# Value product of split probabilities in two passes instead of three, GpSimd's low parts spread, fillers of one attention regrouped

## What is computed

```python
def fox_branch(qb, kb, vb, log_f):
    ...
        logits = jnp.einsum('bqhd,bshd->bhqs', q_blk, kb).astype(jnp.float32) * scale
        logits = logits + jnp.transpose(cq_blk, (0, 2, 1))[..., None] - c_k[:, :, None, :]
        logits = jnp.where(causal[None, None], logits, NEG)
        probs = jax.nn.softmax(logits, axis=-1).astype(vb.dtype)
        return jnp.einsum('bhqs,bshd->bqhd', probs, vb)

def first_block(...):
    ...
    y_a = (att_a * jax.nn.silu(gate_a)) @ w_branch_a[i]
    y_b = (att_b * jax.nn.silu(gate_b)) @ w_branch_b[i]
    m_a, m_b = jnp.split(jax.nn.sigmoid(h @ w_merge[i]), 2, axis=-1)
    out = (m_a * y_a + m_b * y_b) @ w_out[i]
    x = x + rmsnorm(out, g_post[i])
    ...

def second_block(...):
    ...
    o_a = swa_sink_attention(qa, ka, va, swa_sinks[l])
    o_b = mla_attention(q_nope, q_rope, k_nope, k_rope, vb)
    y = jax.nn.sigmoid(g_a) * (o_a @ w_o_swa[l]) + jax.nn.sigmoid(g_b) * (o_b @ w_o_mla[l])
    x = x + y @ w_out[l]
    h = rmsnorm_2(x, ffn_norm_g[l])
    x = x + (jax.nn.silu(h @ w_gate[l]) * (h @ w_up[l])) @ w_down[l]
```

## Time and profile before

| | us |
|---|---|
| median of 3 runs | 1270.14 (1269.06 to 1270.3) |
| the profiled execution | 1270.64 |
| its span | 1268.8 |
| PE busy | 1223.2 (96%) |
| PE weight loads (beside PE) | 1020.5 (80%) |
| DVE busy | 618.7 (49%) |
| ACT busy | 539.7 (43%) |
| POOL busy | 532.7 (42%) |

### The profile page before, as it was taken

The page is one execution under the profiler, slowest core; times in us unless marked ns, Lnnn a source line. Parts: engine busy times, 40 slices in busy tenths (PEclk is TensorE's granted clock), DMA queues, the critical chain, the costliest instruction groups (busy, mean ns, idle before and its releaser), DMA issues.

```text
span 1268.8 us, 15954 instructions
## 1 busy us (share of the span) xinstructions
PE 1223.2 (96%) x6002; PEld 1020.5 (80%) x6002; DVE 618.7 (49%) x1455; ACT 539.7 (43%) x970; POOL 532.7 (42%) x284
## 2 busy tenths in 40 slices
PE   9989899999999989699899999999999999999997
PEld 8868688888888878499789777888788888888886
DVE  5499565673628264874863575582422222130003
ACT  6443473466523354445673466533332222222112
POOL 1436554435443433234353475334344443434441
PEclk9999999999999999799999999999999999999999
DMA  8303661302322423133112300423323233322221
GB/s 263 100 1 117 172 177 67 99 2 67 116 100 67 166 99 100 33 136 118 34 38 67 100 13 22 166 100 100 100 67 102 98 100 100 100 100 97 88 98 67
DMA packets 71115, 119.20 MB, mean 94 GB/s; under 512 B 5624, under 2 KB 33144, under 8 KB 70656
## 3 DMA queue, kind: packets, MB, share of 16 engines
q1 hardware_dynamic: 71040, 118.19, 28.5%
HBM read 107.67 MB, written 4.21 MB: 88 GB/s over the span
## 4 chain that ended last, share of the span: by engine, by line
PE 84%; DVE 7%; POOL 3%; issue 2%; ACT 1%; SPq 1%; DMA 0%; DVEq 0%; ACTq 0%; POOLq 0%
PE bank L1583 63%; PE bank L1865 9%; PE bank L1664 4%; PE bank L1632 2%; PE bank L1646 2%; PE bank L1708 2%; DVE sc L1313 1%; POOL w_lo L665 1%; DVE m L1309 1%; PE bank L1608 1%; DVE tmp L1373 1%; POOL sc L679 1%; ACT w_hi L765 0%; PE bank L1602 0%; SPq L581 0%
## 5 line engine op out<-in xcount | busy, mean ns | idle before, releaser
L648 POOL TENSOR_TENSOR w_lo<-w_raw,w_hi 128x2048 fp32r<-128x2048 f32 (+4 forms) x87 | 383.9, 4412 | 606.7 <-ACT w_hi L732 564.8
L1583 PE MATMUL bank<-aH,w_hi 128*128 128x512 f32 x800 | 318.3, 398 | 9.5 <-DVE aL L1385 3.9
L1583 PE MATMUL bank<-aH,w_lo 128*128 128x512 f32 x800 | 312.9, 391 | 0.0
L1583 PE MATMUL bank<-aL,w_hi 128*128 128x512 f32 x800 | 312.6, 391 | 0.0
L732 ACT ACTIVATE w_hi<-w_raw 128x2048 fp32r<-128x2048 f32 (+4 forms) x83 | 151.8, 1829 | 278.6 <-PE bank L1583 180.7
L1583 PEld LDWEIGHTS bank<-aH,w_hi 128*128 128x128 f32 x800 | 151.1, 189 | 40.1 <-issue 10.9
L1583 PEld LDWEIGHTS bank<-aH,w_lo 128*128 128x128 f32 x800 | 150.5, 188 | 32.4
L1583 PEld LDWEIGHTS bank<-aL,w_hi 128*128 128x128 f32 x800 | 150.9, 189 | 26.5
L1583 PE MATMUL bank<-w_hi,aH 128*128 128x512 f32 (+4 forms) x224 | 78.2, 349 | 7.1 <-ACT aH L961 6.6
L1071 DVE TENSOR_TENSOR fg<-bank,rB 128x512 f32<-128x512 f32 x22 | 15.1, 691 | 127.3 <-PE bank L1583 127.2
L1583 PE MATMUL bank<-w_lo,aH 128*128 128x512 f32 (+4 forms) x224 | 76.6, 342 | 0.0
(11 more groups left out here) (308 smaller groups left out, 2144.7 us busy)
## 6 DMA issues: line engine op xcount, KB each, us to landing
w_raw<-in_w_in SPq DMA_DIRECT2D x23, 1024.0 KB, 5.0
w_raw<-in_w_gate SPq DMA_DIRECT2D x22, 512.0 KB, 3.9
w_raw<-in_w_up SPq DMA_DIRECT2D x22, 512.0 KB, 4.8
w_raw<-in_w_down SPq DMA_DIRECT2D x11, 1024.0 KB, 4.8
w_raw<-in_w_merge SPq DMA_DIRECT2D x8, 1024.0 KB, 4.9
w_raw<-in_w_out SPq DMA_DIRECT2D x8, 1024.0 KB, 5.0
w_raw<-in_w_ple_gate SPq DMA_DIRECT2D x4, 1024.0 KB, 4.8
fK<-kbT SPq DMA_DIRECT2D x24, 128.0 KB, 2.6
```

The costliest lines, as they stand in the source:

```text
L648: pool.tensor_tensor(out=w_lo[:, c % 2, 0:n], in0=w_raw[:, c % 2, 0:n], in1=w_hi[:, c % 2, 0:n].bitcast(F32), op=ALU.subtract).then_inc(w_ ...
L1583: ins = pe.matmul(o, l, r, start=(kk == 0 and m == 0), stop=(kk == total - 1 and m == 2), skip_group_check=True)
```

## The change

Each head's high and low values now stand side by side in the stationary tile, `[high 64 | low 64]`, for one head. It is multiplied with the high probabilities and then with the low ones, two passes into one bank: rows 0 to 63 are high values times both, rows 64 to 127 low values times both. ACT copies rows 64 to 127 into a buffer (`low_rows`), and DVE adds it to rows 0 to 63 into the attention's output (new L1151) and empties the bank, one step after ACT's copy (`i` = 13+4h). For `va` and `vs`, shared by heads, one copy takes the place of two.

POOL's and ACT's units come from two tables: `SIDE_HI` for ACT's halves, `SIDE_LO` for each quarter. fox and dsa stay as they were. In swa both move four and three units ahead, in mla quarters stand at units 12, 13, 16, 17 and 20, 21, 24, 25. In mla mQ's low part stands behind block 2 and mK's behind block 3. In swa ten fillers instead of eight stand before the attention, two of them after the `t.ck` transposes; one filler a unit again from unit 25 and three from unit 32; and the second tile of `t.ck` uses bank 3.

```diff
-SIDE_FIRST = {"fox": 8, "dsa": 8, "swa": 8, "mla": 16}
-SIDE_TAIL = {"fox": (29, 2), "dsa": (29, 2), "swa": (29, 2), "mla": (22, 1)}
-SIDE_SPLIT = {"fox": (20, 27), "dsa": (20, 27), "swa": (20, 27), "mla": (12, 19)}
+SIDE_FIRST = {"fox": 8, "dsa": 8, "swa": 10, "mla": 16}
+SIDE_TAIL = {"fox": ((29, 2),), "dsa": ((29, 2),), "swa": ((25, 1), (32, 2)), "mla": ((22, 1),)}
+SIDE_HI = {"fox": (20, 27), "dsa": (20, 27), "swa": (16, 24), "mla": (11, 19)}
+SIDE_LO = {"fox": ((20, 21, 22, 23), (27, 28, 29, 30)), "dsa": ((20, 21, 22, 23), (27, 28, 29, 30)),
+           "swa": ((16, 17, 18, 19), (24, 25, 26, 27)), "mla": ((12, 13, 16, 17), (20, 21, 24, 25))}
...
-    fill("t.cq", [4, 5, 6]); fill("t.ck", [7, 4])
+    fill("t.cq", [4, 5, 6]); fill("t.ck", [7, 3])
...
-        vbS = place("vbS", 28, [P, 2, NB, S], F32R)
+        vbS = place("vbS", 28, [P, NB, H, 2, DH], F32R)
...
-                    for n, at in enumerate(SIDE_SPLIT[name]):
-                        if at <= i < at + 4:
-                            lo_quarter(UNITS[SIDE[name][1]][0] + n, i - at)
-                    if name == "mla" and b == NB - 2 and h + 2 < H:
+                    for n, at in enumerate(SIDE_LO[name]):
+                        if i in at:
+                            lo_quarter(UNITS[SIDE[name][1]][0] + n, at.index(i))
+                    if name == "mla" and b >= NB - 2 and h + 2 < H:
                         pool.wait_ge(scaled, a.index * NU + i + 1)
-                        split_head(h + 2)
+                        split_head(h + 2, (b - NB + 2,))
...
-                        r = slice(DH * (h % 2), DH * (h % 2) + DH)
+                        if h:
+                            wait_emptied(act, name + ".o", h - 1)
                         wait_filled(act, name + ".o", h)
-                        empties(act.activation(att[r, h // 2, :], bank_of(name + ".o", h)[r, :], ACT.Copy), name + ".o", h)
+                        act.activation(rows[:, :], bank_of(name + ".o", h)[DH:P, :], ACT.Copy).then_inc(rows_moved, 1)
...
-                for i in range(NU + LAG_LO):
+                for i in range(NU + LAG_PV + 2):
+                    if i > LAG_PV + 1 and (i - LAG_PV - 1) % NB == 0:
+                        h = (i - LAG_PV - 1) // NB - 1
+                        dve.wait_ge(rows_moved, a.index * H + h + 1)
+                        empties(dve.tensor_tensor(out=att[DH * (h % 2):DH * (h % 2) + DH, h // 2, :],
+                                                  in0=bank_of(name + ".o", h)[0:DH, :], in1=rows[:, :], op=ALU.add),
+                                name + ".o", h)
...
+            dve.wait_ge(*att_done("mla"))
...
-                            for m, (vp, pp) in enumerate(((0, 0), (0, 1), (1, 0))):
-                                probs = pt[:, pp, at:at + q1 - q0, :].rearrange("p k q -> p (k q)")
-                                ins = pe.matmul(o[:, cols], values(h, kb, vp), probs,
-                                                start=(kb == 0 and m == 0), stop=(kb == 2 and m == 2),
+                            for part_ in range(2):
+                                probs = pt[:, part_, at:at + q1 - q0, :].rearrange("p k q -> p (k q)")
+                                ins = pe.matmul(o[:, cols], values(h, kb).rearrange("p c d -> p (c d)"), probs,
+                                                start=(kb == 0 and part_ == 0), stop=(kb == 2 and part_ == 1),
...
-            side("swa", 4, SIDE_FIRST["swa"])
+            side("swa", 4, 8)
             pe.wait_ge(ql_scaled, 8)
             for j in range(2):
                 turn_tile("t.ck", j, lambda b: kvl[:, b, j * P:(j + 1) * P])
+            side("swa", 8, SIDE_FIRST["swa"])
```

More of the change, by code:

```diff
@@ L205 @@
 SIDE_ALL, SIDE_FROM, SIDE_NEXT = 32, 2, 38
-SIDE_FIRST = {"fox": 8, "dsa": 8, "swa": 8, "mla": 16}
-SIDE_TAIL = {"fox": (29, 2), "dsa": (29, 2), "swa": (29, 2), "mla": (22, 1)}
-SIDE_SPLIT = {"fox": (20, 27), "dsa": (20, 27), "swa": (20, 27), "mla": (12, 19)}
+SIDE_FIRST = {"fox": 8, "dsa": 8, "swa": 10, "mla": 16}
[3 more added lines that the diff above has]
+           "swa": ((16, 17, 18, 19), (24, 25, 26, 27)), "mla": ((12, 13, 16, 17), (20, 21, 24, 25))}
 def side_count(name, i):
-    first, (start, per) = SIDE_FIRST[name], SIDE_TAIL[name]
+    first = SIDE_FIRST[name]
     done = first + min(SIDE_ALL - first, max(0, i - SIDE_FROM + 1))
-    return done + per * max(0, i - start + 1)
+    return done + sum(per * max(0, i - start + 1) for start, per in SIDE_TAIL[name])
 def side_end(name, tile):
@@ L346, in build @@
         kaS = place("kaS", 64, [P, 2, S], F32R)
-        vaS = place("vaS", 68, [P, 2, NB, P], F32R)
+        vaS = place("vaS", 68, [P, NB, 2, DH], F32R)
         sm = place("sm", 94, [P, NB, SM_W])
@@ L352, in build @@
         attB = place("attB", 90, [P, NB, S])
+        low_rows, low_rows2 = place("low_rows", 88, [DH, S]), place("low_rows2", 60, [DH, S])
         attA = place("attA", 98, [P, NB, S])
@@ L695, in split_pair, with split_head @@
                                        op=ALU.subtract).then_inc(pair_lo_ready, 1)
-            def split_head(h):
-                for p, (t, m_) in enumerate(((mqT, mQ), (mkT, mK))):
+            def split_head(h, parts=(0, 1)):
+                for p in parts:
+                    t, m_ = ((mqT, mQ), (mkT, mK))[p]
                     pool.wait_ge(mla_hi_ready, 2 * h + p + 1)
@@ L879, in _ @@
                 wait_filled(act, "vb", b)
-                act.activation(vbS[:, 0, b, :], bank_of("vb", b)[:], ACT.Copy, scale=rT[:, b:b + 1]).then_inc(split_hi, 1)
+                act.activation(vbS[:, b, :, 0, :], bank_of("vb", b)[:].rearrange("p (h d) -> p h d", h=H), ACT.Copy,
+                               scale=rT[:, b:b + 1]).then_inc(split_hi, 1)
             hi_through(UNITS["ga"][0] + 1)
-            exps("fox", sp, pT, attB)
+            exps("fox", sp, pT, low_rows)
             for b in range(NB):
@@ L890, in _ @@
             hi_through(UNITS["m0"][0] + 1)
-            exps("dsa", sp, pT, attA)
+            exps("dsa", sp, pT, low_rows)
             for i in range(8):
@@ L1016, in _ @@
             wait_emptied(act, "t.mq1", 3)
-            exps("mla", sc2, pT2, oB)
+            exps("mla", sc2, pT2, low_rows2)
             for i in range(8):
@@ L1068, in link, with once_low @@
                 dve.wait_ge(dve_step, steps[0])
+            def once_low(dst, hi, src):
+                splits[0] += 1
+                dve.wait_ge(split_hi, splits[0])
+                dve.tensor_tensor(out=dst, in0=src, in1=hi.bitcast(F32), op=ALU.subtract).then_inc(split_lo, 1)
             def mult(o, a, b):
@@ L1331, in fox_bias @@
                 return cB[:, h % 2, 0:(b + 1) * P]
-            softmax("fox", sp, pT, fox_bias)
+            softmax("fox", sp, pT, fox_bias, low_rows, attB)
             top_rounds(ROUNDS_NEXT)
@@ L1343, in _ @@
             softmax("dsa", sp, pT,
-                    lambda h, b: tab("causal")[:, 3 * P:4 * P] if b == 0 else sc[:, span[b][0]:span[b][1]])
+                    lambda h, b: tab("causal")[:, 3 * P:4 * P] if b == 0 else sc[:, span[b][0]:span[b][1]],
+                    low_rows, attA)
             dve.wait_ge(*att_done("fox"))
```

56 lines of the change are left out of this document (30 added, 26 removed).

## The result

The changed kernel takes 1259.46 us (median of 4 runs, 1259.08 to 1260.98), the kernel before 1270.22 us over the runs taken beside it; the ratio is 0.9916, 95% interval 0.9900 to 0.9931. So it is faster by 10.8 us. Forecast were 1250 us, 20 us faster, with a range of 1243 to 1261: the sign and the range held, the gain is half of what the sum gave. The time is that of rival C (1259.6), but that is luck: C had mla gain nothing, and mla gained 5.8 us; most of the error lies in swa, where C had none.

The account below looks back on a forecast made before the run. TensorE was taken as the bound, holding 84% of the chain that ended last. fox -2.2, dsa -4.2, swa -4.8 and mla -8.8 sum to -20.0 us, from the 1270.1 median to 1250 us; range 1243 to 1261.

Parts of the forecast that it names:

- rival C: mla stays at the other engines' pace, so neither its 5.0 us nor its 4.5 us gain appears: 1259.6 us, chance 0.23.
- Value product: One of three passes goes: 0.62 us a head in fox, dsa, mla, 0.45 in swa; together -18.6 us.
- Hand-off: ScalarE's copy, then VectorE's addition of 0.6 to 0.68 us a head, costed at nothing where VectorE has room.
- signs of being wrong: mla's interval above 33 us, VectorE waiting over 0.3 us a head while TensorE idles, or TensorE over 4 us after fox.
- Rival D: Slower: VectorE's in-order wait exposes the hand-off, 1.3 us x 32 heads, 1292 us; sign turns at 0.62 a head; chance 0.05.
- fox and dsa inside: Shortened units in fox and dsa wait for GpSimd's scaling and quarter, about 1.8 us: +0.8 us each.
- After fox: Selection rounds start behind the last additions, so the rotation is late for TensorE: +2.0 us, bounds +0.2 and +4.6.
- swa's start: Two fillers moved to the front and bank 3 for the second t.ck tile remove TensorE's wait: -2.0 us.
- Inside swa: Quarters begin four units earlier, so stalls for scaled rows, 1.8 us in 646 to 656 us, shrink: -0.8 us.
- uq0: Behind swa's last product, without eight covering fillers, it waits for bank 0 through copy, addition and hand-overs: +1.6 us.
- mla: Four heads go from 35.55 to about 28.6 us; of 7.5 us lost, 4.5 return; mla in all -8.8 us.
- Tail of mla: Behind mla the x load waits for the .o bank, emptied later by an addition, and weights follow: +0.7 us.

Follow-up runs that it names:

- experiment 8: The change with every VectorE addition one unit later in VectorE's order; 1255.01 us, ratio 0.9864 to the kernel before.
- experiment 6: The change without VectorE's addition, rows 64 to 127 left out, TensorE's work the same; 1249.57 us, ratio 0.9817 to the kernel before.
- experiment 2: The kernel before with only the change's tables, t.ck bank and fillers, three-pass value product kept; 1265.23 us, ratio 0.9959.
- Experiments 3 and 4: 3: the change with 7 swa fillers behind the last value product again, 1254.11 us; 4: the change with VectorE's n1 gate tiles before its eight copies, 1255.59 us.
- experiment 10: The change with four edits (additions later, 7 fillers behind swa, gate tiles first, two selection rounds earlier), plus mla's second low quarters at units 24 to 27; 1249.14 us.

## Why the prediction was right in part

- **Value product**, right: 0.63 and 0.46 us a head for 0.62 and 0.45. TensorE had it in fox and dsa; these rows decide over the estimate from the gap formula of the Trainium skill, "TensorE: Matmul & The Clock Gate", section "Back-to-back issue gap" (0.54 and 0.38).
- **Hand-off**: the price was right (684 ns for 683). The step "I cost it at nothing where VectorE has room" failed, as the prediction put it "two units of room": it looked at when the bank is needed again and not at what stands behind the addition in VectorE's order. The wait for ScalarE's copy and the addition behind it held the next maximum and low part, also in the stretch where VectorE is busy for 21.45 of 24 us. It cost 2.4 us in swa and mla and 0.4 in fox (experiment 8, with experiment 6 beside it). One of the prediction's signs of being wrong was there: ahead of its additions in fox and mla VectorE waited 0.4 to 2.4 us a head for copied rows (more ahead of the last ones), over its bound of 0.3, though inside fox TensorE idled for 0.2 us in all. Rival D's mechanism was there, at some 0.09 us a head over 32 heads where it would have needed 0.62.
- **fox and dsa inside**, right in size: 4.0 and 3.9 us saved from the first value product to behind the last, for 4.2 (5.0 - 0.8). The 1.8 us that it gives GpSimd for a scaling and a quarter is 0.52 + 1.29 of the earlier trace rows; with the 0.7 that it names, the sum would be 2.0.
- **After fox**, right: +2.0 forecast, 1.75 measured, by the row that was foreseen.
- **swa's start**, right: -0.70 at the first product with two fillers (1.37) more before it is -2.1, for -2.0.
- **Inside swa**, wrong: -0.8 for stalls forecast; idle time between swa's first and last value product went from 1.8 to 3.4 us. The tables alone did take their 0.8 us off (0.96 us in experiment 2). With the shorter product 1.85 us are left even where the addition costs nothing (experiment 8), so 0.9 us of the product's saving turned into waiting for GpSimd's scalings; the addition's place made the other 1.6 us.
- **uq0**, half right: bank 0 at 1.67 us for 1.6. The prediction stopped at the first wait, and this is the largest step that failed. Behind the addition stood eight copies and the gate tile for bank 1, and the chunk that held the copies; 2.27 us, and 1.7 us more of the slower clock behind. Experiments 3 and 4 show both, to 5.4 and 3.9 us.
- **mla**, mis-sized: -7.0 for the four heads (the product's 2.5 and 4.5 of stalls), -4.65 measured. The heads with quarters take 7.83 to 8.47 us whatever the product costs (tables alone: 7.83 and 8.77); the four heads took 30.41 us with the tables and the three-pass product, so none of the product's saving appears in them: rival C's way, in four heads of eight. GpSimd is busy there for 22.51 of 24 us, and where experiment 10 took quarters out of a head, the head got shorter. The count of GpSimd's work, 7.3 us a head, was right as work (22.51/24 of 7.73 us is 7.25) and left out its hand-overs and waits, 0.4 to 0.5 us a head. 0.7 us of the miss is the addition's place.
- **Tail of mla**, the right way and short: 1.3 for 0.7. Without the addition 0.8 us of it goes (experiment 6).

In sum: 7.3 us of the error in swa and 3.0 in mla, against 1.3 us that the profile of before lost to the clock in the index scores.

## What to carry to other kernels

A hand-off that goes through a third engine is priced by its place in that engine's order, not by the slack of its buffer: ask what stands behind the waiting instruction, and put it where its input is ready already. When work is taken from behind a stage, follow every engine's queue to the second and third thing that it must still do for the next stage, and keep a few fillers there as cover. A saving on one engine counts only in the stretches that this engine bounds.
